# Two transformer layers on one core: the second feed-forward's down projection reads its weights 64 bytes lower and its product tiles 64 bytes higher

## What is computed

```
def conv_glu(x, w_gate_up, conv_ffn, w_down):      # x: tokens x 2048
    gu = x @ w_gate_up                             # 2048 x 11264
    gate, up = jnp.split(gu, 2, axis=-1)
    gate = causal_dwconv_2(gate, conv_ffn)
    return (jax.nn.silu(gate) * up) @ w_down       # 5632 x 2048
...
f = conv_glu(rmsnorm(h, g_pre_ffn), w_gate_up, conv_ffn, w_down)
h = h + rmsnorm(f, g_post_ffn)
```

## The kernel before

| operand | in which matmuls | role | address modulo 256, before |
|---|---|---|---|
| `w_hi`, `w_lo` | all projections but ffn2's down | stationary | 128 |
| `act_hi`, `act_lo` | the same | moving | 64 (112 in those of the second input projection that skip the first 12 tokens) |
| `ff_..._rows`, `last_..._rows` | ffn1's down | moving | 64 |
| `w_hi`, `w_lo` | ffn2's down | moving | 128 |
| `ff_..._rows`, `last_..._rows` | ffn2's down | stationary | 64 |

## Time and profile before

### The profile page before, as it was taken

The page is one execution under the profiler, slowest core; times in us unless marked ns, Lnnn a source line. Parts: engine busy times, 40 slices in busy tenths (PEclk is TensorE's granted clock), DMA queues, the critical chain, the costliest instruction groups (busy, mean ns, idle before and its releaser), DMA issues.

```text
span 2471.6 us, 61026 instructions
## 1 busy us (share of the span) xinstructions
PE 2448.8 (99%) x25716; PEld 2360.5 (96%) x25716; DVE 1663.1 (67%) x2174; ACT 1205.5 (49%) x1450; POOL 59.2 (2%) x69
## 2 busy tenths in 40 slices
PE   9999999999999999999999999999999999999999
PEld 9989999999999999999999999999999999999997
DVE  7777767677777777788856655667666666566666
ACT  6656645555555555455523333356444444444444
POOL 0000000000000000004100000001000000000000
PEclk9999999999999999999999999999999999999999
DMA  7555455666566666656533333354656555555553
GB/s 231 172 146 159 149 171 190 194 195 194 189 194 191 191 195 187 195 189 178 158 113 105 97 105 104 105 171 147 211 181 192 181 185 186 187 185 183 184 182 132
DMA packets 397851, 420.57 MB, mean 170 GB/s; under 512 B 15422, under 2 KB 372530, under 8 KB 397554
## 3 DMA queue, kind: packets, MB, share of 16 engines
q1 hardware_dynamic: 397170, 416.46, 54.4%
q10 hardware_dynamic: 528, 1.84, 0.2%
HBM read 416.15 MB, written 2.10 MB: 169 GB/s over the span
## 4 chain that ended last, share of the span: by engine, by line
PE 94%; DVE 3%; ACT 1%; issue 1%; DMA 0%; SPq 0%; ACTq 0%
PE psum L2578 25%; PE psum L2580 25%; PE psum L2579 25%; PE psum L2594 3%; PE psum L2593 3%; PE psum L2592 3%; PE psum L3052 2%; PE psum L3158 1%; DVE w_lo L1384 1%; PE psum L3148 1%; PE psum L3277 0%; PE psum L3199 0%; PE psum L3283 0%; DVE act_lo L1422 0%; PE psum L2824 0%
## 5 line engine op out<-in xcount | busy, mean ns | idle before, releaser
L2578 PE MATMUL psum<-act_hi,w_hi 128*128 128x256 f32 (+2 forms) x4736 | 1346.5, 284 | 4.1 <-DVE act_lo L1422 3.1
L2580 PE MATMUL psum<-act_hi,w_lo 128*128 128x256 f32 (+2 forms) x4736 | 1327.2, 280 | 0.3 <-issue 0.3
L2579 PE MATMUL psum<-act_lo,w_hi 128*128 128x256 f32 (+2 forms) x4736 | 1324.2, 280 | 0.0
L1384 DVE TENSOR_TENSOR w_lo<-raw,w_hi 128x1024 fp32r<-128x1024 f32 x788 | 961.5, 1230 | 464.3 <-ACT w_hi L756 463.6
L756 ACT ACTIVATE w_hi<-raw 128x1024 fp32r<-128x1024 f32 x788 | 829.0, 1057 | 892.0 <-PE psum L2580 749.6
L2578 PEld LDWEIGHTS psum<-act_hi,w_hi 128*128 128x128 f32 x4736 | 889.4, 188 | 12.4 <-issue 3.5
L2579 PEld LDWEIGHTS psum<-act_lo,w_hi 128*128 128x128 f32 x4736 | 893.1, 189 | 3.6 <-issue 2.2
L2580 PEld LDWEIGHTS psum<-act_hi,w_lo 128*128 128x128 f32 x4736 | 889.0, 188 | 0.0
L2578 PE MATMUL psum<-ff_hi_rows,w_hi 128*128 128x256 f32 x640 | 176.6, 276 | 0.0
L2579 PE MATMUL psum<-ff_lo_rows,w_hi 128*128 128x256 f32 x640 | 176.6, 276 | 0.0
L2580 PE MATMUL psum<-ff_hi_rows,w_lo 128*128 128x256 f32 x640 | 176.6, 276 | 0.0
(11 more groups left out here) (429 smaller groups left out, 1922.0 us busy)
## 6 DMA issues: line engine op xcount, KB each, us to landing
raw<-in_w_in SPq DMA_DIRECT2D x188, 512.0 KB, 3.8
raw<-in_w_up SPq DMA_DIRECT2D x176, 512.0 KB, 4.5
raw<-in_w_down SPq DMA_DIRECT2D x176, 512.0 KB, 3.9
raw<-in_w_gate_up SPq DMA_DIRECT2D x176, 512.0 KB, 3.5
raw<-in_w_out SPq DMA_DIRECT2D x64, 512.0 KB, 3.5
x_rows<-in_x SPq DMA_DIRECT2D x8, 256.0 KB, 6.9
out_x<-out_rows SPq DMA_DIRECT2D x8, 256.0 KB, 2.6
raw<-in_w_in SPq DMA_DIRECT2D x4, 384.0 KB, 3.4
```

The source lines that it names most:

```text
L1384: dve.tensor_tensor(w_lo[:, slot], raw[:, slot], w_hi[:, slot].bitcast(F32), ALU.subtract).then_inc(S["lo_done"], 1)
L2578: pe.matmul(out_, wh, xh, start=first and r == 0, stop=False)
L2579: pe.matmul(out_, wh, xl, start=False, stop=False)
L2580: mm = pe.matmul(out_, wl, xh, start=False, stop=last and r == RK - 1)
```

## The change

No instruction is added, removed or put elsewhere in any engine's order: the five engines have the same instructions with the same waits before and after, and the same shapes. These places in SBUF change:

- The slots of `w_hi` and `w_lo` grow by 256 bytes (`W_STEP`, 4352 bytes). A unit is written 64 bytes into its slot, or at the slot's start where it is a unit of ffn2's down projection (`weights(..., down=True)`). The address modulo 256 stays 128 for all units but those, and becomes 64 for those.
- The product tiles lie at the start of `ff_hi_rows` and its three sisters in ffn1, as before, and 16 elements (64 bytes) further in ffn2. There the address modulo 256 goes from 64 to 128.
- Room is made for it: `rstd` and `ss_part` lie ahead of `w_hi`, a pad is made smaller, the scan's small tiles `ld` and `p` lie in `ss_part`, which is free at that time, and `gate_b` is 12 columns narrower. The large operands of the table above keep their address modulo 256; slots 1 and 3 of the weights shift by 256 modulo 512, `act_hi` and `act_lo` both by 256 modulo 512.

```diff
+    W_STEP = RK * 256 + 64
...
-    w_hi = sb("w_hi", [P, NSLOT, RK * 256], F32R)
-    w_lo = sb("w_lo", [P, NSLOT, RK * 256], F32R)
+    rstd = sb("rstd", [P, T2])
+    ss_part = sb("ss_part", [P, T2])
+    norm_rows = ss_part[0:KD, 0:P]
+    sb("w_pad", [P, 16])
+    w_hi = sb("w_hi", [P, NSLOT * W_STEP], F32R)
+    w_lo = sb("w_lo", [P, NSLOT * W_STEP - 48], F32R)
+
+    def weights(t, slot, down=False):
+
+        at = W_STEP * slot + (0 if down else 16)
+        return t[:, at:at + RK * 256]
...
-    sb("act_pad", [P, 56])
+    sb("act_pad", [P, 24])
...
-        *[(n, [4, RC], F32) for n in ("ldt", "lo", "rbt0", "rbt1", "akt", "rkt0", "rkt1", "ld", "p")],
+        *[(n, [4, RC], F32) for n in ("ldt", "lo", "rbt0", "rbt1", "akt", "rkt0", "rkt1")],
...
-        ("gate_b", [2, T2], F32), ("gate_c", [2, T2], F32),
+        ("gate_b", [2, TS], F32), ("gate_c", [2, T2], F32),
...
+    for g, n in enumerate(("ld", "p")):
+        M[n] = ss_part[:, P * g:P * g + P].rearrange("p (h t) -> p h t", t=RC)
+
+    FF_AT = dict(ffn1=0, ffn2=16)
+
+    def ff_rows(name, ff):
+
+        at = FF_AT[name]
+        return [M[t][:, at:at + 4 * T1].rearrange("p (k t) -> p k t", t=T1)
+                for t in (ff + "_hi_rows", ff + "_lo_rows")]
...
-                act.activation(w_hi[:, slot], raw[:, slot], ACT.Copy).then_inc(S["hi_done"], 1)
+                act.activation(weights(w_hi, slot, down), raw[:, slot], ACT.Copy).then_inc(S["hi_done"], 1)
...
-                dve.tensor_tensor(w_lo[:, slot], raw[:, slot], w_hi[:, slot].bitcast(F32),
+                dve.tensor_tensor(weights(w_lo, slot, down), raw[:, slot],
+                                  weights(w_hi, slot, down).bitcast(F32),
                                   ALU.subtract).then_inc(S["lo_done"], 1)
...
-                    wh, wl = w_hi[:, slot, at:at + m], w_lo[:, slot, at:at + m]
+                    wh, wl = [weights(t, slot)[:, at:at + m] for t in (w_hi, w_lo)]
...
-                    wh = w_hi[:, slot, 512 * r:512 * r + 512]
-                    wl = w_lo[:, slot, 512 * r:512 * r + 512]
+                    wh, wl = [weights(t, slot, True)[:, 512 * r:512 * r + 512]
+                              for t in (w_hi, w_lo)]
...
-                    downs(u + 24 * i + 8, gp * i - (gp - 8) + g0, i - 1, FF_HI, FF_LO)
+                    downs(u + 24 * i + 8, gp * i - (gp - 8) + g0, i - 1, *ff_rows(name, "ff"))
```

More of the change, by code:

```diff
@@ L163, in two_blocks @@
     halves = sb("halves", [P, P])
-    rstd = sb("rstd", [P, T2])
-    ss_part = sb("ss_part", [P, T2])
-    norm_rows = ss_part[0:KD, 0:P]
     head_par = sb("head_par", [P, 6])
@@ L749, in _, with hi @@
         def _(act):
-            def hi(u, slot):
+            def hi(u, slot, down=False):
                 act.wait_ge(landed[slot], 16 * (u // 4 + 1) if isinstance(u, int)
@@ L766, in landed_at, with hi_group @@
                 return (u - slot) * 4 + 16
-            def hi_group(u):
+            def hi_group(u, down=False):
                 for j in range(4):
-                    hi(u + j, j)
+                    hi(u + j, j, down)
             def square(name, src, sq, j, tc):
@@ L994, in ffn @@
                 nt = 8 if vals else 4
+                down = not vals
                 K1 = len(cc) - 1
@@ L1026, in while_up @@
                     hi_group(v + 8)
-                    product_hi(i - 1, v, FF_HI)
+                    product_hi(i - 1, v, ff_rows(name, "ff")[0])
                     hi(v + 12, 0)
@@ L1045, in ffn @@
                     while_up(i, v)
-                    hi_group(v + 16)
-                    hi_group(v + 20)
+                    hi_group(v + 16, down)
+                    hi_group(v + 20, down)
                 i = FCH - 1
@@ L1050, in ffn @@
                 while_up(i, w - 16, last=True)
-                hi(w, 0)
-                hi(w + 1, 1)
+                hi(w, 0, down)
+                hi(w + 1, 1, down)
                 if vals:
                     silu(i)
-                hi(w + 2, 2)
-                hi(w + 3, 3)
+                hi(w + 2, 2, down)
+                hi(w + 3, 3, down)
                 if vals:
@@ L1060, in ffn @@
                     first_taps(i, range(4, nt))
-                hi(w + 4, 0)
-                hi(w + 5, 1)
+                hi(w + 4, 0, down)
+                hi(w + 5, 1, down)
                 if not vals:
@@ L1065, in ffn @@
                 for k in range(2, 5):
-                    hi(w + 4 + k, k % 4)
-                product_hi(i, None, LAST_HI)
+                    hi(w + 4 + k, k % 4, down)
+                product_hi(i, None, ff_rows(name, "last")[0])
                 for k in range(5, 8):
-                    hi(w + 4 + k, k % 4)
+                    hi(w + 4 + k, k % 4, down)
                 ending(w + 12, g0 + 12 * FCH - 7)
@@ L1090, in rows_end @@
                     if n in (0, 2):
-                        hi(w + n, n)
-                        hi(w + n + 1, n + 1)
+                        hi(w + n, n, True)
+                        hi(w + n + 1, n + 1, True)
                     act.wait_ge(S["last_left"], n + 1)
@@ L1380, in _, with lo @@
         def _(dve):
-            def lo(u, slot):
+            def lo(u, slot, down=False):
                 dve.wait_ge(S["hi_done"], u + 1)
-                dve.tensor_tensor(w_lo[:, slot], raw[:, slot], w_hi[:, slot].bitcast(F32),
+                dve.tensor_tensor(weights(w_lo, slot, down), raw[:, slot],
+                                  weights(w_hi, slot, down).bitcast(F32),
                                   ALU.subtract).then_inc(S["lo_done"], 1)
@@ L1865, in leave_rows, with downs_leave @@
                           how="added")
-                def downs_leave(v, d):
+                def downs_leave(v, d, last=False):
                     if not by_rows:
@@ L1872, in downs_leave @@
                     else:
-                        lo(v + 4 + d, d % 4)
+                        lo(v + 4 + d, d % 4, d < 4 or last)
                         if d % 2 == 0:
@@ L1890, in while_up @@
                             taps(i, 2 * j - 2, 2)
-                    product_lo(i - 1, FF_HI, FF_LO)
+                    product_lo(i - 1, *ff_rows(name, "ff"))
                     leave_up(v, 2)
                     for j in range(3):
-                        lo(v + 16 + j, j)
+                        lo(v + 16 + j, j, by_rows)
                     leave_up(v, 3)
-                    lo(v + 19, 3)
+                    lo(v + 19, 3, by_rows)
                 if by_rows:
@@ L1932, in ffn @@
                 for d in range(8):
-                    downs_leave(w, d)
+                    downs_leave(w, d, True)
                     if vals and d < 4:
@@ L1938, in ffn @@
                     elif d == 5:
-                        product_lo(i, LAST_HI, LAST_LO)
+                        product_lo(i, *ff_rows(name, "last"))
                 ending(w, pair0, leave_down)
@@ L1955, in rows_end @@
                     if g < 2:
-                        lo(w + 12 + 2 * g, 2 * g)
+                        lo(w + 12 + 2 * g, 2 * g, True)
                     dve.wait_ge(S["unit_used"], w + 10 + 2 * g)
@@ L1961, in rows_end @@
                     if g < 2:
-                        lo(w + 13 + 2 * g, 2 * g + 1)
+                        lo(w + 13 + 2 * g, 2 * g + 1, True)
                     if g < 3:
@@ L2204, in leave_loop @@
                         dve.wait_ge(S["cv_done"], q)
-                    leave(v, side_pair(n), gate_b[:, :, TCS], TS, t0=SKIP)
+                    leave(v, side_pair(n), gate_b[:], TS, t0=SKIP)
                 elif kind == "c":
@@ L2231, in conv_taps @@
                 dve.wait_ge(S["cv_step"], 7 * q + 7)
-                dve.tensor_tensor(y[:, :, TCS], y[:, :, TCS], gate_b[:, :, TCS], ALU.mult) \
+                dve.tensor_tensor(y[:, :, TCS], y[:, :, TCS], gate_b[:], ALU.mult) \
                     .then_inc(S["cv_done"], 1)
@@ L2967, in ffn @@
                         mm.then_inc(S["h_rows"], 1)
-                downs(u + 24 * FCH - 8, g0 + gp * FCH - (gp - 4), FCH - 1, LAST_HI, LAST_LO)
+                downs(u + 24 * FCH - 8, g0 + gp * FCH - (gp - 4), FCH - 1,
+                      *ff_rows(name, "last"))
                 if by_rows:
@@ L3334, in _ @@
                         at = 256 * r + P * c
-                        wh, wl = w_hi[:, 2 + j, at:at + P], w_lo[:, 2 + j, at:at + P]
+                        wh, wl = [weights(t, 2 + j)[:, at:at + P] for t in (w_hi, w_lo)]
                         k = 8 + 4 * j + r
```

## The result

| | before | after |
|---|---|---|
| median of 12 executions | 2473.45 us | 2479.71 us |
| lowest and highest | 2470.39, 2478.68 us | 2475.55, 2482.71 us |
| ratio, with its 95% interval | | 1.0023 (1.0014 to 1.0032) |

The change makes the kernel slower by 0.23%, or 5.7 us of 2473.45, with an interval of 3.5 to 7.9 us; the two medians lie 6.3 us apart. The median after lies 0.7 us above the top of my range, and the case with the most weight, a gain of 2.5 us, did not come about.

The account below looks back on a forecast made before the run. The prediction took TensorE's matmul pitch to bound the kernel. ffn2's down matmuls were to save 2.5 us and all else cost nothing, so the median 2473.61 us became 2471.1 us, with a range of 2464.0 to 2479.0 us.

Parts of the forecast that it names:

- my range: Whole kernel: 2464.0 to 2479.0 us, leaving out the flips and the worst of the less dense case.
- the case with the most weight: ffn2's down chunks: pitch 226.7 ns, 21.76 us a chunk, 2.5 us less in all, 2471.1 us; chance 0.33.
- What bounds the kernel: Whole kernel: TensorE, busy 99% of the span, so time can only come from how densely its matmuls follow each other.
- the stationary and moving operands of ffn2's down matmuls: 1056 matmuls in 11 ffn2 down chunks: from 9.6 us less to 6.9 us more, 2.5 us less taken.
- The first, that nothing happens: ffn2's down chunks: swapped placement is a mirror image, so nothing changes, 21.99 us a chunk, 2473.6 us; chance 0.28.
- The second rival: ffn2's down matmuls: surplus per matmul, 220.0 ns, 9.6 us less, 2464.0 us; chance 0.22 including pitches up to 224.4 ns.
- The third, slower: ffn2's down chunks fall into the less dense rhythm: 235.6 ns, 6.9 us more, 2480.5 us; chance 0.10.
- The costs put at nothing: Weight units' writes by ACT and DVE, shifted slots and activations, and the scan's `ld`, `p` and `gate_b`: no time added.
- The flip elsewhere: Stream from 417 to 1097 us takes the less dense rhythm: 26.7 us more, 2498 us; chance 0.04 for the worse.
- My own sign of being wrong: ffn2's down matmuls: pitch outside 224.4 to 233.8 ns; also a changed first feed-forward rhythm or new TensorE waits.

Follow-up runs that it names:

- The first runs: Changed kernel with ffn2's down operands back at old places: 21.98 us a chunk, ratio 1.000; with only tiles moved 21.77 us, only weights moved 21.80 us.
- half the change: Changed kernel with the weights put back, only the product tiles moved (both at 128): 2472.34 us against 2474.85 us for the kernel before, ratio 0.999.

## Why the prediction was wrong

**What bounds the kernel** was right. The 4.5 us of the chunks are all TensorE's pitch, with no wait in them, and no other engine matters there. The view that I chose, the distance between starts, is the one that shows it.

**The step that failed** is the price of "the stationary and moving operands of ffn2's down matmuls". I took 226.7 ns, twice ffn1's pitch for 256 columns, because ffn1's down matmuls have the new placement (moving 64, stationary 128). The measured pitch is 233.3 ns. The first runs and the one with all weights at 64 show what was wrong in it: the good placement for 256 columns (difference 64, 113.3 ns against 120.0 at 0) is the bad one for 512 (233.3 ns against 226.7 at 0). A pitch was carried over from one column count to another because the addresses were the same. The trace before could have warned of it: 260 columns have 118.7 ns at a difference of 16 and 120.0 ns at 64, so that the place that I took for the good one was the worse of the two there. The figure of 226.7 ns itself does exist, at a difference of 0, where half the change would have led: 0.999 of the time before, the 2.5 us of my forecast.

**The rivals.** The first, that nothing happens because before and after are mirror images, fell: modulo 128 they are, modulo 256 they are differences of 192 and 64, with 21.99 and 22.40 us. Beside it I set a rule of the Trainium skill ("TensorE: Matmul & The Clock Gate", section "Step-by-step: what each phase is for"), that a load takes no bandwidth from the running matmul. The runs do not agree with it for this stream: with the stream's operand left alone, the place of what the load reads changed the chunk from 21.80 to 22.40 us, and a load that reads one column changed it from 22.40 to 22.24 us. The second rival, one surplus for each matmul (21.12 us a chunk), was seen in no run. The third, slower, came nearest: it gave 22.62 us a chunk and 2480.5 us, against 22.40 us and 2479.71 us. That the total is so near is in part luck, since the chunks account for 4.5 us and this rival for 6.9. It also named the wrong mechanism. It spoke of a rhythm into which the stream may fall at this placement, and of 235.6 ns; the measured rhythm is one of its own, the same in every chunk and every profile at this difference. I gave it 0.10.

**The costs put at nothing** were right as far as can be told: the writes have their old lengths, and with the old pair of places the new layout gives a ratio of 1.000 (0.9991 to 1.0009). The flip elsewhere did not happen either. The 6000 matmuls from 417 to 1097 us kept 113.3 ns in the profile after.

**The range** missed by 0.7 us. Its upper part was cut at 2479.0 although the bound from the rows was 2480.5, on the ground that this end was unlikely. The chunks explain 4.5 us, which added to the median before is 2478.0 us and inside the range; the rest is within the scatter, as the ratio's interval of 3.5 to 7.9 us holds 4.5. So the miss of the range by 0.7 us is partly chance, and the miss of the direction is not. My own sign of being wrong, a pitch outside 224.4 to 233.8 ns, did not catch it: 233.3 ns is inside, because those bounds stood for 0.2% of the time and not for the mechanism.

**Open** is the mechanism. Difference modulo 256, column count and what the load reads all count, and the stream is locked in repeating patterns (226, 229 and 232 ns before, 231 and 236 ns after, 226 and 227 ns at a difference of 0). That two reads of SBUF get in each other's way fits, but no run shows such a meeting directly, and what I forecast from it for the load of one column (216 to 227 ns with the tiles at 128, 22.23 us a chunk with them at 64) failed both times, at 231.7 ns and 21.98 us.

## What to carry to other kernels

In a stream of float32r matmuls that is TensorE-bound, the start addresses of the two operands are worth up to 6%: measure the pitch (distance of starts in the timeline) for each column count by itself at stationary minus moving of 0, 64, 128 and 192 bytes modulo 256, and take for each stage its own best. Where one placement shows two rhythms, look at every stretch between interruptions. Do not carry the best placement from one column count to another, nor move both operands when one would do; here each half of the change was a gain and the whole a loss. When a price is taken from a row of another shape, keep the row's worst rhythm inside the range too.

## What the runs showed of the hardware

Pitch of float32r matmuls with a 128-column load each, at full granted clock, by stationary minus moving address modulo 256 bytes. What the columns alone take is their number over 2.4 GHz.

| columns | alone | 0 | 16 | 32 | 64 | 96 | 128 | 192 |
|---|---|---|---|---|---|---|---|---|
| 256 | 106.7 ns | 120.0 | | | 113.3 or 117.8 | | | |
| 260 | 108.3 ns | 118.7 or 120.0 | 118.7 or 120.0 | | 120.0 | 120.0 | 120.0 or 121.1 | |
| 272 | 113.3 ns | 125.2 to 126.7 | | | 123.2 to 124.0 | | | |
| 512 | 213.3 ns | 226.7 | | 233.3 | 233.3 | | 232.3 to 233.3 | 229.1 |

In the second layer the activations step by 1280 bytes from one tile to the next, a multiple of 256 and not of 512, so what the table says of 260 and 272 columns holds for addresses in both halves of 512 bytes. A difference of 208 (the same matmuls as at 16, in the version with the whole second layer at 64) gives 260 columns 119.0 to 119.5 ns.

I had not expected that the difference of the two addresses is what acts, that its best value is not the same for all column counts, that for 512 columns 32 bytes do as much as 64, nor that a stream whose loads read a single column still has most of its surplus (229.0 or 231.7 ns for 512 columns, depending on where the load starts).
